# A hybrid decoder step on one core: projections behind two norms take centred, unscaled tiles, and the inverse deviation is applied to their results

## The chip, the core and the metric

One core of one Trainium2 chip runs the whole program. The metric is the device time of one execution in microseconds (us); smaller is better. Engines are named as in the profile: PE is TensorE (PEld its weight loads), DVE is VectorE, ACT is ScalarE, POOL is GpSimd, SP is SyncE, which issues the loads of the weights.

## What is computed

One inference step of a two-layer decoder for 256 prompt tokens and 8 sample tokens, with shared weights, in float32. The model width is 1024. Layer 0 is a gated DeltaNet mixer and a dense SwiGLU, layer 1 a short gated convolution and a mixture of eight experts. After each of the four parts the residual stream is normalised:

```
x = layer_norm(ALPHA * x + mixer(x))        # (x - mean) * rsqrt(var + 1e-5) * g + b
swiglu(x)    = (silu(x @ W_gate) * (x @ W_up)) @ W_down           # W_gate, W_up: 1024 x 2816
shortconv(x) = (B * conv3(C * h)) @ W_out,  [B, C, h] = x @ W_in  # W_in: 1024 x 3072
```

The change concerns two of the norms: that between the DeltaNet mixer and the SwiGLU (norm 0), whose result feeds `W_gate` and `W_up`, and that between the SwiGLU and the short convolution (norm 1), whose result feeds `W_in`.

## The kernel before

Activations lie transposed: 8 tiles `k` of 128 model rows by N = 264 columns (256 prompt and 8 sample tokens), in `xres`. Each fp32 product is made of three fp32r products: weights and activations are split into a high part (rounded to fp32r) and a low part (the rest), and high x high, high x low and low x high are summed. Weights come in slots of 1 MB. SP loads them up to seven slots ahead (`load`, L322 to L329, waits for the slot that had the place), ACT makes the high half of a slot (`split_high`, L331 to L336, three places, so slot n + 3 waits for slot n), DVE the low half (`split_low`, L338 to L342). PE works through a slot in `dense_slot` (L344 to L365): two output tiles, 16 products with the high half and 8 with the low half for each, 48 in all, and then raises `slot_used`.

The program is a written order for each engine; semaphores tie them. The stages are numbered by slot: four slots of `W_out` of the DeltaNet mixer (from `OUT0`), 22 of gate and up (`GU0`; pair i is a gate slot and an up slot of 256 columns each), 11 of `W_down` (`DOWN0`), 8 of C and h in pairs and 4 of B (`SCI0`), 4 of the convolution's `W_out` (`SCO0`), and then the experts (`MOE0`).

At norm l the order is a chain through three engines. DVE adds the residuals (L1183). PE sums the eight tiles against a matrix of ones, in 16 instructions, as each fp32 product is two (L1721). DVE makes `mu` (L1200) and subtracts it from each tile (L1203); ACT squares (L811); PE sums the squares (L1725); ACT makes `rstd` with a logarithm and an exponential, with the load of an activation table between them (L813, L815). Then, tile by tile, DVE scales by g and `rstd` (L1211), ACT adds b and rounds to `xh` (L818), DVE makes `xl` (L1207), and PE multiplies (L355, L356). ACT adds b to `xres` at the end (L821), for the next residual.

In the gate and up stage ACT applies silu to the gate bank (L838), DVE multiplies with the up bank (L1229), ACT and DVE split the product into `hh` and `hl` (L842, L1232), and both work on the sample states beside it: ACT scales the eight tiles of `dB` (L848), DVE updates `s0f` (L1239). In pairs 0, 1 and 2 PE also transposes eight blocks of `utail` into the banks of the next up slot (L1742) and waits until ACT has copied them out (L832, `tail_rows` after the change). The down stage starts when `hl` is complete. POOL starts the loads of the sample states when `xres` is final (L538).

## Time and profile before

| | us |
|---|---|
| median of 3 runs (1663.86 to 1668.59) | 1667.0 |
| the profiled execution | 1664.93 |
| its span, first to last instruction | 1663.2 |
| PE busy in the span | 1577.7 (95%) |
| DVE busy | 1273.1 (77%) |
| ACT busy | 1054.9 (63%) |
| POOL busy | 98.6 (6%) |

PE is the engine to look at: the share of the others is an average over stages with different limits. Matmuls are pipelined: a row gives the time from the start of the first to the modelled end of the last, so the distance between two starts is the price of what lies between them. Times of rows are us from the start of the span.

### The profile page before, as it was taken

What the parts mean: (1) busy time and instruction counts of PE and PEld (TensorE: products, weight loads), DVE (VectorE), ACT (ScalarE), POOL (GpSimd) and SP (SyncE); (2) the same over time, 40 slices, a digit from 0 to 9 for tenths busy, and PEclk for the clock granted to TensorE, in tenths of its full rate; (3) what the DMA queues carried; (4) which work ended last, traced back from release to release, by engine and by line L of the source; (5) the groups of instructions that cost most, each with busy time, mean ns of one, the idle gap of its engine ahead of it and who ended that gap; (6) DMA issues with size and microseconds to landing.
All of it is one profiled execution on the core that took longest, in us unless ns stands there. A gap on an engine that the chain in (4) does not pass through costs nothing.

```text
span 1663.2 us, 23648 instructions
## 1 busy us (share of the span) xinstructions
PE 1577.7 (95%) x8965; PEld 1367.2 (82%) x8965; DVE 1273.1 (77%) x1237; ACT 1054.9 (63%) x961; POOL 98.6 (6%) x155
## 2 busy tenths in 40 slices
PE   8899988999998999999999999999999999999991
PEld 7789987899997998887887887887887887887881
DVE  5786554567445758889889889889889889889887
ACT  5984233666334335777777777777777777777772
POOL 3105000121000011000000000000000000002001
PEclk9999998999998999999999999999999999999996
DMA  9747603598454545999999999999999999999991
GB/s 274 217 129 263 229 3 113 163 313 296 169 179 139 179 164 186 385 368 352 383 367 350 384 364 353 380 368 350 384 363 357 381 361 361 377 364 360 394 361 65
DMA packets 228401, 480.26 MB, mean 289 GB/s; under 512 B 9756, under 2 KB 69164, under 8 KB 228041
## 3 DMA queue, kind: packets, MB, share of 16 engines
q1 hardware_dynamic: 217000, 439.33, 74.1%
q0 software_dynamic: 11344, 40.12, 7.0%
q8 instruction: 41, 0.67, 0.2%
q14 instruction: 16, 0.13, 0.0%
HBM read 452.88 MB, written 26.77 MB: 288 GB/s over the span
## 4 chain that ended last, share of the span: by engine, by line
PE 88%; ACT 5%; DVE 4%; issue 1%; DMA 1%; DVEq 0%; SPq 0%; POOL 0%; ACTq 0%; POOLq 0%
PE bank L1866 13%; PE bank L1870 13%; PE bank L1867 13%; PE bank L1895 12%; PE bank L355 6%; PE bank L364 6%; PE bank L356 6%; PE bank L1901 6%; ACT high L336 2%; PE bank L1758 1%; PE bank L1759 1%; PE bank L1623 1%; PE bank L1764 1%; PE bank L1644 1%; PE bank L1878 1%
## 5 line engine op out<-in xcount | busy, mean ns | idle before, releaser
L341 DVE TENSOR_TENSOR low<-raw,high 128x2048 fp32r<-128x2048 f32 x408 | 931.1, 2290 | 244.3 <-ACT high L336 244.1
L336 ACT ACTIVATE high<-raw 128x2048 fp32r<-128x2048 f32 x408 | 779.8, 1917 | 284.3 <-PE bank L1870 103.2
L1866 PE MATMUL bank<-high,xgh 128*128 128x512 f32 x896 | 359.2, 401 | 0.7 <-DVE xgl L1419 0.7
L1867 PE MATMUL bank<-high,xgl 128*128 128x512 f32 x896 | 355.1, 396 | 0.0
L355 PE MATMUL bank<-xh,high 128*128 128x264 f32 x864 | 233.5, 301 | 15.6 <-ACT xh L818 7.7
L1870 PE MATMUL bank<-low,xgh 128*128 128x512 f32 x896 | 246.0, 396 | 0.0
L356 PE MATMUL bank<-xl,high 128*128 128x264 f32 x864 | 225.5, 293 | 0.0
L1870 PEld LDWEIGHTS bank<-low,xgh 128*128 128x128 f32 x896 | 168.9, 189 | 41.4
L1866 PEld LDWEIGHTS bank<-high,xgh 128*128 128x128 f32 x896 | 169.1, 189 | 39.5 <-issue 0.9
L1867 PEld LDWEIGHTS bank<-high,xgl 128*128 128x128 f32 x896 | 168.5, 188 | 38.7
L355 PEld LDWEIGHTS bank<-xh,high 128*128 128x128 f32 x864 | 169.8, 197 | 20.7 <-issue 20.7
L356 PEld LDWEIGHTS bank<-xl,high 128*128 128x128 f32 x864 | 170.4, 197 | 1.0 <-issue 1.0
L1895 PE MATMUL bank<-high,hth 128*128 128x512 f32 x448 | 141.4, 397 | 8.1 <-DVE htl L1435 8.1
L1895 PE MATMUL bank<-high,htl 128*128 128x512 f32 x448 | 140.5, 395 | 0.0
L364 PE MATMUL bank<-xh,low 128*128 128x264 f32 x864 | 129.8, 291 | 0.8 <-DVE low L341 0.8
L1901 PE MATMUL bank<-low,hth 128*128 128x512 f32 x448 | 122.3, 394 | 0.0
L364 PEld LDWEIGHTS bank<-xh,low 128*128 128x128 f32 x864 | 116.1, 193 | 1.1 <-DVE low L341 1.1
L1895 PEld LDWEIGHTS bank<-high,hth 128*128 128x128 f32 x448 | 83.5, 188 | 28.8 <-issue 10.0
L1901 PEld LDWEIGHTS bank<-low,hth 128*128 128x128 f32 x448 | 84.4, 188 | 20.2
L1895 PEld LDWEIGHTS bank<-high,htl 128*128 128x128 f32 x448 | 84.5, 189 | 19.8
L913 ACT ACTIVATE sgx<-bank 128x512 f32<-128x512 f32 x56 | 33.5, 598 | 42.6 <-PE bank L1870 42.5
L618 POOL TENSOR_TENSOR flag<-flag 128x1 f32<-128x1 f32 x1 | 2.3, 2255 | 873.7 <-DMA tok<-ysb 873.7
(370 smaller groups left out, 1463.9 us busy)
## 6 DMA issues: line engine op xcount, KB each, us to landing
raw<-in_moe_w_gu_dram SPq DMA_DIRECT2D x224, 1024.0 KB, 5.3
raw<-in_moe_w_down_dram SPq DMA_DIRECT2D x115, 1024.0 KB, 5.4
raw<-in_ffn_w_gu_dram SPq DMA_DIRECT2D x22, 1024.0 KB, 5.5
raw<-in_gdn_w_in_dram SPq DMA_DIRECT2D x16, 1024.0 KB, 9.1
tok<-zeros POOLq DMA_DIRECT2D x26, 512.0 KB, 18.2
raw<-in_sc_w_in_dram SPq DMA_DIRECT2D x12, 1024.0 KB, 5.0
raw<-in_ffn_w_down_dram SPq DMA_DIRECT2D x11, 1024.0 KB, 5.1
tok<-ysb SPq DMA_DIRECT2D x9, 512.0 KB, 5.9
```

The costliest lines, as they stand in the source:

```text
L336: eng.activation(high[:, n % SPLIT, :], raw[:, n % RAW, :], ACT.Copy).then_inc(high_ready, 1)
L341: eng.tensor_tensor(low[:, n % RAW, :], raw[:, n % RAW, :], high[:, n % SPLIT, :].bitcast(F32), ALU.subtract).then_inc(low_ready, 1)
L355: pe.matmul(out, wh[:, k, f], act_h[:, k, :], start=k == 0, stop=False)
L356: pe.matmul(out, wh[:, k, f], act_l[:, k, :], start=False, stop=False)
L364: last = pe.matmul(out, wl[:, k, f], act_h[:, k, :], start=False, stop=k == KT - 1)
L913: act.activation(sgx[:, u % 2, :], bank[2 * (u % 2)][:, :], ACT.Silu).then_inc(sgx_ready, 1)
L1623: last = pe.matmul(heads(4 * c + g)[:, h % 4, :], AT[:, c, h, :], T[:, c, h, :], start=True, stop=True)
L1866: pe.matmul(out, xgh[:, 4 * kh + k, :], wh[:, k, :], start=kh + k == 0, stop=False)
L1867: pe.matmul(out, xgl[:, 4 * kh + k, :], wh[:, k, :], start=False, stop=False)
L1870: last = pe.matmul(out, xgh[:, 4 * kh + k, :], wl[:, k, :], start=False, stop=kh == 1 and k == 3)
L1895: pe.matmul(bank[4 + g][:, :], src[:, u % 2, hs], wh[:, k, 512 * g:512 * g + 512], start=u + kh + k == 0 and src is hth, stop=False)
L1901: last = pe.matmul(bank[4 + g][:, :], hth[:, u % 2, hs], wl[:, k, 512 * g:512 * g + 512], start=False, stop=u == UNITS - 1 and kh + k == 2)
```

## The change

For a norm with z = x - mean, the projection W(z * rstd * g + b) is rstd * W(z * g) + W b, since `rstd` belongs to a column (a token) and not to a row. The kernel after uses this:

- The activation tiles get two more columns that hold b (N = 264, WIDE = 266), so that column 264 of each result is W b. `xh` and `xl` become the halves of z * g, made before the variance is known.
- The first slot behind each norm runs through `first_slot`, which goes by tile k through all products with `xh` first (two outputs, high and low weights), and then those with `xl`. The sum of squares follows this slot on PE.
- DVE multiplies each result by `rstd` out of the bank, and the column of W b is added in the silu (as its bias), in the identity of the C part, or in a `scalar_tensor_tensor` (up, h and B parts).
- `xres` is scaled by DVE (`norm_scale`) and shifted by ACT (`norm_shift`) later: two tiles in each of pairs 0 to 3 for norm 0, and around the slots of the convolution's `W_out` for norm 1.
- Most sums of the mean move into the slot before the norm. All `utail` transposes but the last eight come ahead of the first gate slot. POOL starts the state loads at the sums of the mean.
- ACT splits the next block before the gate work; DVE makes `hl` a pair later, except for the last pair; the first four banks of the down stage no longer wait for `hl` of the last pair; the last down slot is done output by output, so that residuals run beside it.
- In the convolution ACT makes the first of the three taps; the sums for `sgb` go behind the first slot of `W_out`, and that slot waits for `yl` tile by tile.

The core of the diff (sizes and places of the wide tiles, and the plain mirror lines of other stages, are left out):

```diff
+        def first_slot(pe, n, b, l):
...
+            for k in range(KT):
+                pe.wait_ge(xh_ready, halves_base(l) + k + 2)
+                for t in range(2):
+                    f = slice(128 * t, 128 * t + 128)
+                    pe.matmul(bank[b + t][:, 0:WIDE], wh[:, k, f], xhb[:, k, :], start=k == 0, stop=False)
+                    pe.matmul(bank[b + t][:, 0:WIDE], wl[:, k, f], xhb[:, k, :], start=False, stop=False)
+            for k in range(KT):
+                pe.wait_ge(xl_ready, halves_base(l) + k + 2)
+                for t in range(2):
+                    f = slice(128 * t, 128 * t + 128)
+                    last = pe.matmul(bank[b + t][:, 0:WIDE], wh[:, k, f], xlb[:, k, :], start=False, stop=k == KT - 1)
+            last.then_inc(slot_used, 1)
...
@@ gpsimd
-            pool.wait_ge(x_new, 8)
+            pool.wait_ge(mean_psum, 1)
@@ scalar
+            def norm_halves(l):
+                act.activation(xhb[:, :, N:WIDE], vecs[:, :, 4 + l:5 + l].to_broadcast([128, KT, 2]), ACT.Copy).then_inc(xh_ready, 1)
                 for k in range(KT):
                     act.wait_ge(xc_ready, 8 * l + k + 1)
+                    act.activation(xh[:, k, :], xres[:, k, :], ACT.Copy, scale=vecs[:, k, l:l + 1]).then_inc(xh_ready, 1)
+                for k in range(KT):
                     act.activation(lnsq[:, k, :], xres[:, k, :], ACT.Square).then_inc(lnsq_ready, 1)
...
+            norm_halves(0)
             act.wait_ge(hist_out, 48)
+            tail_rows(0)
+            tail_rows(1)
+            norm_scale(0)
             for i in range(FF // 256):
                 n = GU0 + 2 * i
+                if i == 2:
+                    tail_rows(2)
                 act.wait_ge(slot_used, n + 1)
                 split_high(act, n + SPLIT)
                 for t in range(2):
+                    act.wait_ge(gate_scaled, 2 * i + t + 1)
+                    g = sg[:, 2 * (i % 2) + t, :]
+                    act.activation(g[:, 0:N], g[:, 0:N], ACT.Silu, bias=g[:, N:N + 1]).then_inc(gate_silu, 1)
+                act.wait_ge(slot_used, n + 2)
+                if i < FF // 256 - 1:
+                    split_high(act, n + 1 + SPLIT)
+                    hidden_high(i)
+                else:
+                    hidden_high(i)
+                    split_high(act, n + 1 + SPLIT)
+                if i < KT // 2:
+                    norm_shift(0, 2 * i)
+                    norm_shift(0, 2 * i + 1)
                 if 1 <= i <= HEADS:
                     h = i - 1
                     act.wait_ge(sf_in[h % 2], 32 * (h // 2 + 1))
...
@@ vector
+            norm_halves(0)
+            split_low(dve, GU0 - 1 + SPLIT)
+            dve.wait_ge(var_root, 1)
             for i in range(FF // 256):
                 n = GU0 + 2 * i
                 dve.wait_ge(slot_used, n + 1)
+                for t in range(2):
+                    dve.tensor_tensor(sg[:, 2 * (i % 2) + t, :], bank[4 * (i % 2) + t][:, 0:WIDE], rstd[:, :], ALU.mult)\
+                        .then_inc(gate_scaled, 1)
+                if i:
+                    hidden_low(i - 1)
                 split_low(dve, n + SPLIT)
                 dve.wait_ge(slot_used, n + 2)
+                for t in range(2):
                     r = 2 * (i % 2) + t
+                    step(dve.tensor_tensor(hf[:, r, :], bank[4 * (i % 2) + 2 + t][:, 0:WIDE], rstd[:, :], ALU.mult))
+                step.wait()
+                for t in range(2):
+                    dve.wait_ge(gate_silu, 2 * i + t + 1)
+                    r = 2 * (i % 2) + t
+                    dve.scalar_tensor_tensor(hf[:, r, 0:N], hf[:, r, 0:N], hf[:, r, N:N + 1], sg[:, r, 0:N], ALU.add, ALU.mult)\
+                        .then_inc(h_ready, 1)
+                if i == FF // 256 - 1:
+                    hidden_low(i)
                 split_low(dve, n + 1 + SPLIT)
+                if i < KT // 2:
+                    norm_scale(0, 2 * i)
+                    norm_scale(0, 2 * i + 1)
...
@@ tensor
+                dense_slot(pe, n, 2 * (n % 2), xh, xl, out_arrives if n == OUT0 else None,
+                           half=(lambda: mean_sums(0, 0, 6)) if n == GU0 - 1 else None)
+            mean_sums(0, 6, KT)
...
             for i in range(FF // 256):
+                if i == 1:
+                    pe.wait_ge(var_inv, 1)
                 if i >= 2:
+                    pe.wait_ge(gate_scaled, 2 * (i - 1))
                     pe.wait_ge(h_ready, 2 * (i - 1))
+                for j in ((0, 1), (), (2,))[i] if i < 3 else ():
...
+                if i == 0:
+                    first_slot(pe, GU0, 0, 0)
+                    variance_sums(0)
+                else:
+                    dense_slot(pe, GU0 + 2 * i, 4 * (i % 2), xhb, xlb)
                 if i < 3:
+                    pe.wait_ge(tail_sb, 2 * (i + 1))
+                dense_slot(pe, GU0 + 2 * i + 1, 4 * (i % 2) + 2, xhb, xlb)
-            pe.wait_ge(hl_ready, FT)
             for n in range(DOWN0, SCI0):
...
+                pe.wait_ge(hl_ready, f + 2)
+                if n == SCI0 - 1:
+                    pe.wait_ge(low_ready, n + 1)
+                    for d in range(KT):
...
+                        last.then_inc(down_psum if d < KT - 1 else slot_used, 1)
+                        if d == KT - 2:
+                            pe.wait_ge(res_ready, 8 + 5)
+                            mean_sums(1, 0, 5)
+                    continue
+                for d in (4, 5, 6, 7, 0, 1, 2, 3):
+                    if n == DOWN0 and d in (4, 0):
+                        pe.wait_ge(h_ready, FT - 2 if d == 4 else FT)
...
```

DVE's `norm_halves` makes the low half of the two b columns (after a wait for ACT's first instruction above), `mu`, the eight centred tiles, and then the eight tiles of `xl` as `(x * g) - xh`. In the last slots before both norms ACT's `split_high` stands ahead of `norm_halves` in its order, as before.

## Rows read from the trace of the kernel before

**Rows 1.** The page: the chain that ended last, share by engine.

```profile
PE 88%; ACT 5%; DVE 4%; issue 1%; DMA 1%; DVEq 0%; SPq 0%; POOL 0%; ACTq 0%; POOLq 0%
```

**Rows 2.** Windows: stretch, length, busy us and instructions per engine, granted clock, DMA share, GB/s.

```profile
497.00:520.00 23.00, 14.37 (x49) 10.64 (x49) 14.83 (x34) 13.29 (x25) 0.11 (x1) 0.78 0.15 47
```

**Rows 3.** Timeline of PE and PEld at norm 0: start, length, line, idle before.

```profile
278.49 3.42 PEld L1721 LDWEIGHTS bank<-xres,ones 128*128 128x128 f32 x16
278.61 3.72 PE L1721 MATMUL bank<-xres,ones 128*128 128x264 f32 x16
284.45 5.51 PE L1725 MATMUL bank<-lnsq,ones 128*128 128x264 f32 x16 [2.12 <-ACT lnsq L811]
294.10 0.36 PE L355 MATMUL bank<-xh,high 128*128 128x264 f32 x1 [3.26 <-ACT xh L818]
...
310.15 0.86 PEld L1742 LDWEIGHTS bank<-ident,utail 128*11 128x11 f32 x8
```

**Rows 4.** Timeline of DVE and ACT at norm 0.

```profile
278.81 0.77 DVE L1183 SCALAR_TENSOR_TENSOR xres<-xres,bank 128x264 f32<-128x264 f32 x2 [1.53 <-PE bank L364]
283.05 0.42 DVE L1200 TENSOR_SCALAR mu<-bank 128x264 f32<-128x264 f32 x1
283.51 2.84 DVE L1203 TENSOR_TENSOR xres<-xres,mu 128x264 f32<-128x264 f32 x8
297.51 1.29 DVE L1207 SCALAR_TENSOR_TENSOR xl<-xres,vecs,xh 128x264 fp32r<-128x264 f32 x3
...
278.89 1.91 ACT L336 ACTIVATE high<-raw 128x2048 fp32r<-128x2048 f32 x1 [3.94 <-PE bank L364]
283.98 2.82 ACT L811 ACTIVATE lnsq<-xres 128x264 f32<-128x264 f32 x8 [1.87 <-DVE xres L1203]
290.50 1.28 ACT L815 ACT_TABLE_LOAD   x1
298.05 3.34 ACT L821 ACTIVATE xres<-xres,vecs 128x264 f32<-128x264 f32 x8
```

**Rows 5.** Timeline of DVE and ACT in pairs 1 and 2.

```profile
323.05 0.77 DVE L1229 TENSOR_TENSOR hf<-sg,bank 128x264 f32<-128x264 f32 x2 [0.99 <-PE bank L364]
326.11 2.29 DVE L341 TENSOR_TENSOR low<-raw,high 128x2048 fp32r<-128x2048 f32 x1 [1.37 <-ACT high L336]
328.45 2.19 DVE L1239 SCALAR_TENSOR_TENSOR s0f<-s0f,aS,dB 128x128 f32<-128x128 f32 x8
...
325.98 2.44 ACT L848 ACTIVATE dB<-dB,kS 128x128 f32<-128x128 f32 x8
328.32 1.05 ACT L832 ACTIVATE tail_nat<-bank 11x512 f32<-11x512 f32 x2
```

**Rows 6.** Timeline of PE at the start of the down stage.

```profile
428.23 1.13 PE L364 MATMUL bank<-xh,low 128*128 128x264 f32 x8
431.14 0.43 PE L1758 MATMUL bank<-hh,high 128*128 128x264 f32 x1 [1.78 <-DVE hl L1232]
438.64 0.29 PE L1758 MATMUL bank<-hh,high 128*128 128x264 f32 x1
```

**Rows 7.** Timeline of PE around norm 1 and before the slots of `SCO0`.

```profile
491.21 0.29 PE L1758 MATMUL bank<-hh,high 128*128 128x264 f32 x1
531.49 0.29 PE L355 MATMUL bank<-xh,high 128*128 128x264 f32 x1
591.12 1.04 PE L1781 MATMUL bank<-ident,su 128*10 128x128 f32 x8 [0.86 <-DVE sy L1289]
591.99 1.86 PE L1785 MATMUL bank<-gbw,ones 128*128 128x16 f32 x16
```

**Rows 8.** Windows of two us with the granted clock.

```profile
286.00:288.00 2.00, 2.00 (x6) 1.52 (x5) 0.34 (x1) 0.80 (x3) 0.00 (x0) 0.50 0.00 0
505.00:507.00 2.00, 0.55 (x3) 0.19 (x2) 1.56 (x5) 0.66 (x2) 0.00 (x0) 1.00 0.00 0
```

**Rows 9.** Chain in order of time, in the experts: start, length, what.

```profile
669.00 1.86 PE bank L1895 x8
```

More of the change, by code:

```diff
@@ L11 @@
 N = NP + NS
+WIDE = N + 2
 HEADS = 8
@@ L350, in dense_slot @@
                 f = slice(128 * t, 128 * t + 128)
-                out = bank[b + t][:, 0:N]
+                out = bank[b + t][:, 0:act_h.shape[2]]
                 for k in range(KT):
@@ L360, in dense_slot @@
                     pe.wait_ge(low_ready, n + 1)
+                elif half is not None:
+                    half()
                 for k in range(KT):
@@ L824, in _, with norm_shift, tail_rows @@
-            layer_norm(0)
+                act.activation(rstd[:, 0:N], rvar[:, :], ACT.Exp, scale=-0.5).then_inc(var_root, 1)
+            def norm_shift(l, k):
+                act.wait_ge(scaled, 8 * l + k + 1)
+                act.activation(xres[:, k, :], xres[:, k, :], ACT.Identity, bias=vecs[:, k, 4 + l:5 + l]).then_inc(x_new, 1)
+            def tail_rows(i):
+                for t in range(2):
+                    act.wait_ge(tail_psum, 2 * i + t + 1)
+                    act.activation(tail_nat[:, 1024 * i + 512 * t:1024 * i + 512 * t + 512],
+                                   bank[tail_bank(i) + t][0:11, :], ACT.Copy).then_inc(tail_sb, 1)
@@ L876, in _ @@
                 split_high(act, n + SPLIT)
+                for k in range(2 * (n - SCO0) + 2, min(2 * (n - SCO0) + 4, KT)):
+                    norm_shift(1, k)
             act.preload_act_table_set("natural_log")
@@ L1285, in _ @@
                 for t in range(2):
[L1286 to L1289 removed]
+                    step(dve.tensor_tensor(sy[:, 2 * (i % 2) + t, :], bank[2 * i + t][:, 0:WIDE], rstd[:, :], ALU.mult))
+                step.wait()
+                for t in range(2):
+                    f, y = 2 * i + t, sy[:, 2 * (i % 2) + t, :]
+                    dve.scalar_tensor_tensor(y[:, 0:N], y[:, 0:N], y[:, N:N + 1], sc[:, f, :], ALU.add, ALU.mult).then_inc(sy_ready, 1)
+                if i < D // 256 - 1:
+                    split_low(dve, n + SPLIT)
                 for t in range(2):
@@ L1302, in _ @@
             for n in range(SCO0, MOE0):
+                for k in range(2 * (n - SCO0) + 2, min(2 * (n - SCO0) + 4, KT)):
+                    norm_scale(1, k)
                 dve.wait_ge(slot_used, n + 1)
+                dve.wait_ge(x_new, 8 + 2 * (n - SCO0) + 2)
                 for t in range(2):
@@ L1710, in out_arrives, with mean_sums @@
                     pe.wait_ge(xl_ready, 8 + 4 + k // 2 + 1)
+            def mean_sums(l, first, end):
+                for k in range(first, end):
+                    pe.wait_ge(res_ready, 8 * l + k + 1)
+                    last = pe.matmul(bank[4][:, 0:N], ones[:, :], xres[:, k, :], start=k == 0, stop=k == KT - 1)
+                if end == KT:
+                    last.then_inc(mean_psum, 1)
             for n in range(OUT0, GU0):
@@ L1782, in _ @@
                 last.then_inc(stail_psum, 1)
-            pe.wait_ge(const_ready, 7)
-            for k in range(KT):
-                last = pe.matmul(bank[7][:, 0:16], ones[:, :], gbw[:, k, :, :].rearrange("p a e -> p (a e)"),
-                                 start=k == 0, stop=k == KT - 1)
-            last.then_inc(sgb_psum, 1)
             def row_tiles(k):
```

253 lines of the change are left out of this document (132 added, 121 removed).

## The prediction

> **What bounds the kernel now.** I read the chain that ended last first: PE holds 88% of it [rows 1]. In the gate, down and expert stages PE runs on end, and a cheaper DVE or ACT step there buys nothing. What can be bought is where PE waits, so I went through windows and then timelines for gaps. Before norm 1 and its first slot PE is busy 14.37 of 23.00 us, at a mean granted clock of 0.78 [rows 2]. Norm 0 looks the same [rows 3], the down stage starts with a short gap [rows 6], and one stands before the slots of `SCO0` [rows 7]. At a norm two things cost: the chain PE, DVE, ACT, PE, ACT, DVE, ACT, PE, and the clock, which falls to half (1.2 GHz) behind such gaps.
>
> **Unit prices on PE.** Nine down slots follow one another from 438.64 to 491.21 [rows 6, 7]: 52.57 / 9 = 5.84 us a slot of 48 products, 0.122 a product at 2.4 GHz. The first down slot took 438.64 - 431.14 = 7.50 [rows 6], 1.66 more: its first 16 products ran at 1.2 GHz, 0.10 more each, so a product costs 0.220 there. A sum instruction of a norm costs (3.72 - 0.39) / 15 = 0.222 at full clock (0.39 is the modelled drain of the last) [rows 3].
>
> **Norm 0.** I put zero at 278.49, where the low products of the last slot are out [rows 3]. Before, eight transposes end at 310.15 + 0.86 = 311.01, where pair 1 begins: 32.5 us. After:
> - Twelve sum instructions stand inside the last slot, 12 x 0.222 = 2.7, so the slot ends at 2.7. The residuals follow 0.32 later (278.81 - 278.49) and take 0.77 [rows 4]: 3.8. The last two sums end at 4.4. This alone gains nothing: the sums were hidden beside the residuals, and now the residuals wait for them.
> - ACT's `split_high` stands ahead of its first new instruction, from 3.1 to 5.0 (0.40 behind the slot's end, 1.91 long [rows 4]). The b columns on ACT and DVE cost 0.2 and 0.3 (small operations; none of this shape is in the rows, and L1200 at 0.42 bounds each from above, zero from below). `mu` starts at 5.5, before it was 283.05 - 278.49 = 4.6.
> - First centred tile 0.46 behind (283.51 - 283.05), ACT 0.47 behind that, PE 0.55 behind that (lnsq took 284.45 - 283.98 = 0.47; a scaled copy is some 0.08 longer) [rows 3, 4]: products from 7.0. The 16 transposes (2 x 0.86) fill 4.4 to 6.1, so PE has two short gaps of 1.0.
> - 32 products with `xh`, 3.9 at full clock: 10.9. ACT gives a tile each 3.34 / 8 = 0.42 [rows 4], PE eats four products per tile in 0.49: PE is the slower. `xl`: DVE is free at 5.9 + 2.84 = 8.8, and eight at (1.29 - 0.49) / 2 = 0.40 [rows 4] end at 12.0; PE ends at 12.3.
> - 16 sums, 3.6: 15.9. Up slot, 5.84: 21.7. `rstd` comes 2.3 behind the sums, beside that slot, and the table load of 1.28 [rows 4] is hidden there.
> Gain 32.5 - 21.7 = **10.8**. If the clock falls in these gaps, 17 `xh` products run at 0.220 and the `xl` products no longer wait for DVE: 14.5 instead of 12.3, a loss of 2.2. Nearest rows: a gap of 1.45 in the window at 505 left the clock at 1.00 [rows 8]; the gap of 2.12 at norm 0 was followed by 0.50 [rows 3, 8]. Gaps of 1.0 are nearer to the first; I take full clock.
>
> **Pairs 0 to 3.** ACT's order is now: split, two copies of `hh`, two shifts of `xres`, eight `dB`, and only then, at the head of pair 2, the copies of `tail_rows(2)`. The shifts wait for DVE's scaling, which stands behind a low split. PE waits for these copies before the up slot of pair 2. With zero at the end of pair 1's up slot: DVE `hf` from 0.3, 0.77 [rows 5]; `scalar_tensor_tensor` twice at 0.40, to 2.0; ACT's high half 0.3 to 2.2; low half 2.29 [rows 5], to 4.5; scales 4.9 and 5.4; shifts to 5.8; `dB` 2.44 less an overlap, to 8.2; copies 1.05, to 9.3 [rows 5]. PE is there at 0.86 + 5.84 = 6.7. **A stall of 2.5** in place of none: before, the same copies ended at 328.32 + 1.05 = 329.37, just when they were due. It is a gap longer than that of 1.78 at the down stage, behind which 16 products ran at 0.220 [rows 6]; I take 1.5 more for the clock. Bounds: 1.5 less each if DVE is quicker by its overlaps or the clock stays up. **Loss 4.0.**
> Nothing else of the stage reaches PE. DVE's round for pairs 1 to 3 is 0.77 + 0.78 + 2.29 + 0.77 + 0.85 + 2.29 + 0.85, then a wait for `dB` (2.4 + 0.4), then 2.19 [rows 5]: 13.6 against PE's 11.7. It falls behind by 1.9 a pair, but its latest product, the low half of slot n + 4, is due two slots and 16 products, 13.6, after the up slot and done at 4.5 plus the lag; the cover is 9, the lag at most 6, and from pair 4 the round is 11.0. `hl` a pair later costs nothing, for that reason. The last `utail` transposes stand before and after. State loads 20 us earlier meet idle DMA queues.
>
> At this point a rule of the Trainium skill would matter. No row shows a silu directly ahead of an identity; if identity lay outside silu's table, each of these pairs would pay 1.28 twice (the load row at 290.50 [rows 4]), and the stall would grow by 1.3. ScalarE: Activation LUTs, Table sets, says that cheap functions such as identity stand in every set; by it the term is zero.
>
> **Down stage.** Before, the low products of the last up slot are out at 428.23 + 8 x 0.122 = 429.21, the second down slot starts at 438.64: 9.43, 3.59 over 5.84 [rows 6]. After, 16 products (1.95) on banks 4 to 7 cover `hf` 0.3 + 0.77 and the two following, to 2.0. **Gain 3.4.**
>
> **Norm 1.** Zero at 491.21; before, 40.3 to 531.49 [rows 7]. After: seven outputs of six products, 5.1; ten sums, 7.3; the last output, 8.1; four sums beside the last residual, then two: 9.4. Here the residuals do run beside products. ACT's `split_high` again decides: 8.3 to 10.2, b columns to 10.8, then 0.46 + 0.47 + 0.55: products from 12.3. PE has idled 2.8 without transposes, so I take the low clock for 17 products as at the down stage: 12.3 + 3.7 + 1.8 = 17.8; 16 with `xl`, 19.8; sums, 23.3; slot, 29.2. **Gain 11.1**; 13.3 if the clock stays up (bounded then by `xl` at 17.3), 8.1 if it stays low through the first slot, as it did there before.
>
> **Behind it.** At `SCO0` the gap of 0.86 [rows 7] goes; the sums of `sgb` (1.7) only move behind the first slot; the last `yl` now holds tiles 6 and 7 by 0.3. **Gain 0.7** with rounding. `norm_scale` and `norm_shift` of norm 1 lie in idle time of DVE and ACT in the 5.84 of a slot; nobody waits before `SCO0 + 2`.
>
> **Wider tiles.** 34 slots x 48 products have two columns more. Rows: 8 products of 512 columns start (1.86 / 8) 0.2325 apart [rows 9], against 0.122 for 264: 0.445 ns a column, 0.9 ns a product, 1632 of them: **loss 1.45**.
> By TensorE: Matmul & The Clock Gate, Back-to-back issue gap, of the Trainium skill (N / 2.4 ns plus a constant), the loss is an estimated 1.36; its 112 ns for 264 columns is below the 122 of this trace.
>
> **Sum.** 10.8 - 4.0 + 3.4 + 11.1 + 0.7 - 1.45 = 20.5 us. The profiled execution took 1664.93 us, 1.7 above its span; 1664.9 - 20.5 = 1644.4. It lay 2.1 below the median of the three runs, 1667.0, so the median after is 1646.5. 0.3% (5 us) is about what a measurement of this kernel can tell from no change.
>
> **Rivals.**
> 1. The clock stays up and ACT reaches the copies in time: plus 2.2 (norm 1), plus 1.5 to 4.0 (pair 2): 1640.3 to 1642.8. For it: the gaps are short. Against it: both are longer than the 2.12 that was enough.
> 2. The clock falls at norm 0 too (2.2) and stays low through the first slot of norm 1 (3.0): 1651.7. For it: before norm 1 did just that; but there PE was fed by DVE at half load, now it is not.
> 3. Identity reloads tables: 1647.8 and up.
> 4. DVE becomes the bound of the gate and up stage. It now reads four banks a pair where it read two. If a read beside PE's writes cost double (1.54 more a pair), the round would be 15.1 in pairs 1 to 3 and 12.5 in pairs 4 to 8, over 11.7 by 3 x 3.4 + 5 x 0.8 = 14.2; less the cover of 9, 5 us: 1651.7. Against it: `hf`, with a bank operand, costs 0.77 for two, little more than tile operations without one (0.36 to 0.40 each) [rows 4, 5].
> 5. Slower: the width of 266 takes the products off their rate. The rows of such products have 264 or 512 columns, both multiples of eight. If the wide products of slots `GU0` to `SCO0` ran as slowly as the sums of the norms (0.222 for 264 columns), they would lose 1632 x 0.10 = 163 us: 1809. It outweighs the rest from 22 / 1632 = 0.0135 us a product. Against it: 264 and 512 columns both run at about 2.2 columns a ns (264 / 0.122, 512 / 0.2325), and nothing in the instruction changes but its count.
>
> **Chances.** Forecast 0.55 (its own range 1643.5 to 1649.5), rival 1 0.17, rival 2 0.15, rival 3 0.05, rival 4 0.04, rival 5 0.04; of rival 5 a quarter ends within 0.3%, and something unnamed may eat the gain. Faster 0.93, same 0.04, slower 0.03. The range for 8 in 10 takes in most of rivals 1 and 2: 1640 to 1653.
>
> **What would show it.** First `first_slot` product 7 us behind the moved origin at norm 0, without `rstd` before it; a PE gap of 2.5 in pair 2 released by ACT's `tail_rows`; no gap at the down stage; at norm 1 a gap of 2.8, `mu` right behind ACT's split, and a granted clock of 0.50 behind it; products of 266 columns 0.9 ns further apart. Wrong would be: PE waiting in pairs 3 to 10, which is DVE's round; or an unchanged gap before `SCO0`.

## The result, and the profile after

The changed kernel takes 1638.49 us (median of 4 runs, 1637.19 to 1639.28); the kernel before, in the runs made with it, 1667.8 (4 runs). The ratio is 0.983, 95% interval 0.981 to 0.985. Forecast were 1646.5 and a range down to 1640.0: the sign is right, the gain is larger than the range allows. The profiled execution took 1639.28 us against 1664.93 before. That is 25.65 us less, where the sum had 20.5. The missing 5 us are the question of this study.

The page of the kernel after (span 1637.6 us): busy time of each engine, and the chain that ended last, by engine.

```profile
PE 1560.2 (95%) x8965; PEld 1358.1 (83%) x8965; DVE 1295.6 (79%) x1301; ACT 1061.2 (65%) x971; POOL 100.2 (6%) x155
...
PE 87%; ACT 6%; DVE 4%; issue 1%; DMA 1%; DVEq 0%; SPq 0%; ACTq 0%; POOLq 0%
```

PE still holds the chain [rows 1]. The shares say nothing of where the time went, so I read the stages one by one, each from the same event in both traces.

**Norm 0**, timelines of PE, DVE and ACT (start, length, what, idle before and its releaser), against [rows 3, 4]:

```profile
278.04 2.84 PE L1816 MATMUL bank<-xres,ones 128*128 128x264 f32 x12
282.38 1.16 PE L1816 MATMUL bank<-xres,ones 128*128 128x264 f32 x4 [0.52 <-DVE xres L1247]
285.82 0.36 PE L359 MATMUL bank<-xhb,high 128*128 128x266 f32 x1 [0.53 <-ACT xhb L845]
289.84 2.14 PE L365 MATMUL bank<-xlb,high 128*128 128x266 f32 x16
291.82 3.72 PE L1830 MATMUL bank<-lnsq,ones 128*128 128x264 f32 x16
301.32 0.28 PE L379 MATMUL bank<-xhb,high 128*128 128x266 f32 x1
...
281.98 1.91 ACT L341 ACTIVATE high<-raw 128x2048 fp32r<-128x2048 f32 x1 [6.63 <-PE bank L390]
284.23 0.43 DVE L1269 TENSOR_SCALAR mu<-bank 128x264 f32<-128x264 f32 x1
```

The twelve sums stand ahead of the slot's last eight products (0.98 us) now. The zero of the prediction, the moment at which PE would be through the slot without them, is therefore 278.04 + 0.98 = 279.02. Pair 1 starts at 301.32, 22.3 behind; before it was 311.01 - 278.61 = 32.4 [rows 3]. The gaps of PE are 0.52 and 0.53, and the 32 products with `xhb` take 4.02 (285.82 to 289.84), so the clock stayed up.

**Pair 2**, timeline of PE, then windows (length; busy us and instructions of PE, PEld, DVE, ACT, POOL; granted clock; DMA share, GB/s):

```profile
318.99 1.15 PE L390 MATMUL bank<-xhb,low 128*128 128x266 f32 x8
322.41 0.59 PE L379 MATMUL bank<-xhb,high 128*128 128x266 f32 x1 [2.28 <-ACT tail_nat L863]
...
322.00:324.00 2.00, 1.59 (x7) 1.59 (x8) 2.00 (x9) 2.00 (x2) 1.15 (x3) 0.53 1.05 364
324.00:326.00 2.00, 2.00 (x13) 2.00 (x13) 2.00 (x4) 0.97 (x3) 0.87 (x1) 0.62 0.83 222
```

This is the foreseen stall, released by `tail_rows`, with the foreseen fall of the clock behind it. From 322.41 to the next slot at 329.82 it takes 7.41 us, where the slots of later pairs take 5.92: 1.5 us for the clock.

**Down stage and norm 1**, timelines of PE, DVE and ACT, against [rows 6, 7]:

```profile
423.56 1.15 PE L390 MATMUL bank<-xhb,low 128*128 128x266 f32 x8
424.54 0.28 PE L1877 MATMUL bank<-hh,high 128*128 128x264 f32 x1
...
485.72 2.29 DVE L346 TENSOR_TENSOR low<-raw,high 128x2048 fp32r<-128x2048 f32 x1 [3.90 <-ACT high L341]
487.93 2.46 DVE L1247 SCALAR_TENSOR_TENSOR xres<-xres,bank 128x264 f32<-128x264 f32 x7
489.76 2.49 PE L1816 MATMUL bank<-xres,ones 128*128 128x264 f32 x10 [1.37 <-DVE xres L1247]
492.82 1.50 PE L1816 MATMUL bank<-xres,ones 128*128 128x264 f32 x6
493.11 1.91 ACT L341 ACTIVATE high<-raw 128x2048 fp32r<-128x2048 f32 x1 [7.84 <-PE bank L1866]
495.33 0.43 DVE L1269 TENSOR_SCALAR mu<-bank 128x264 f32<-128x264 f32 x1
496.92 0.36 PE L359 MATMUL bank<-xhb,high 128*128 128x266 f32 x1 [2.59 <-ACT xhb L845]
500.93 2.14 PE L365 MATMUL bank<-xlb,high 128*128 128x266 f32 x16
512.41 0.28 PE L379 MATMUL bank<-xhb,high 128*128 128x266 f32 x1
```

The down stage starts right behind the last gate products. In its last slot DVE works on a low half (485.72 to 488.01) while seven banks wait for their residuals, and PE idles 1.37 us for it. The ten sums were meant to be hidden there. After the gap of 2.59 the 32 products take 4.01 (496.92 to 500.93), at full clock.

**Experts.** Their code is the same. Rows of one line, its first and last start: eight transposes of `xrow` for each of eight jobs, of before and then of after.

```profile
L1835 PE MATMUL bank<-ident,xrow x64: 272/273/273, 761.1 to 1622.4; 128*128 128x128 f32 x64
```

```profile
L1963 PE MATMUL bank<-ident,xrow x64: 272/273/273, 740.1 to 1596.6; 128*128 128x128 f32 x64
```

Seven periods took 861.3 us before and 856.5 after: 123.04 a job against 122.36. The chain in order of time (start, length, what) shows where, against [rows 9]:

```profile
647.67 0.93 PE bank L1998 x4
648.60 1.85 PE bank L2023 x8
650.45 0.91 PE bank L2029 x4
651.36 1.81 PE bank L2023 x8
```

Up products (L1998) need what they needed; down products (L2023, L2029), which have `hth` or `htl` as weights, are a little quicker: 1.81 to 1.85 for eight against 1.86. Over all 1344 of them, the median distance of two starts is 227 ns against 232; for the 2688 up products it is 234 in both traces. The granted clock is 1.00 in both. From the first expert product to the last instruction it makes 1012.1 us against 1017.4.

### The profile page after: what moved, and what is told of

Its sections match the earlier page's. It is cut to its first block, busy times and chain, and to the rows that moved or that the text cites. A ratio compares the mean times of both kernels' runs of the same rounds, so it can differ in the third digit from the quotient of the medians.

```text
span 1637.6 us, 23706 instructions
## 1 busy us (share of the span) xinstructions
PE 1560.2 (95%) x8965; PEld 1358.1 (83%) x8965; DVE 1295.6 (79%) x1301; ACT 1061.2 (65%) x971; POOL 100.2 (6%) x155
## 4 chain that ended last, share of the span: by engine, by line
PE 87%; ACT 6%; DVE 4%; issue 1%; DMA 1%; DVEq 0%; SPq 0%; ACTq 0%; POOLq 0%
PE bank L1995 13%; PE bank L1994 13%; PE bank L1998 13%; PE bank L2023 12%; PE bank L379 6%; PE bank L390 6%; PE bank L380 6%; PE bank L2029 6%; ACT high L341 2%; DVE low L346 1%; PE bank L1724 1%; PE bank L1745 1%; PE bank L2006 1%; PE bank L1877 1%; PE bank L1878 1%
## 5 line engine op out<-in xcount | busy, mean ns | idle before, releaser
L1998 PE MATMUL bank<-low,xgh 128*128 128x512 f32 x896 | 245.7, 396 | 0.0
L379 PE MATMUL bank<-xhb,high 128*128 128x266 f32 (+1 forms) x832 | 222.5, 299 | 10.3 <-ACT xhb L823 7.6
L380 PE MATMUL bank<-xlb,high 128*128 128x266 f32 (+1 forms) x832 | 215.7, 290 | 0.0
L1998 PEld LDWEIGHTS bank<-low,xgh 128*128 128x128 f32 x896 | 168.9, 188 | 41.1
L379 PEld LDWEIGHTS bank<-xhb,high 128*128 128x128 f32 x832 | 162.1, 195 | 12.5 <-issue 9.4
L380 PEld LDWEIGHTS bank<-xlb,high 128*128 128x128 f32 x832 | 161.4, 194 | 1.1 <-issue 1.0
L2023 PE MATMUL bank<-high,hth 128*128 128x512 f32 x448 | 140.0, 394 | 8.7 <-DVE htl L1536 8.7
L2023 PE MATMUL bank<-high,htl 128*128 128x512 f32 x448 | 138.6, 391 | 0.0
L390 PE MATMUL bank<-xhb,low 128*128 128x266 f32 (+1 forms) x832 | 124.8, 290 | 1.3 <-DVE low L346 1.3
L2029 PE MATMUL bank<-low,hth 128*128 128x512 f32 x448 | 119.9, 389 | 0.0
L390 PEld LDWEIGHTS bank<-xhb,low 128*128 128x128 f32 x832 | 110.8, 191 | 1.7 <-DVE low L346 1.6
L2023 PEld LDWEIGHTS bank<-high,hth 128*128 128x128 f32 x448 | 83.5, 188 | 28.2 <-issue 10.6
L2023 PEld LDWEIGHTS bank<-high,htl 128*128 128x128 f32 x448 | 84.1, 188 | 18.8
L2029 PEld LDWEIGHTS bank<-low,hth 128*128 128x128 f32 x448 | 84.1, 188 | 18.1
## 6 DMA issues: line engine op xcount, KB each, us to landing
raw<-in_gdn_w_in_dram SPq DMA_DIRECT2D x16, 1024.0 KB, 10.1
```

What stands on the lines that cost most here:

```text
L379: pe.matmul(out, wh[:, k, f], act_h[:, k, :], start=k == 0, stop=False)
L380: pe.matmul(out, wh[:, k, f], act_l[:, k, :], start=False, stop=False)
L390: last = pe.matmul(out, wl[:, k, f], act_h[:, k, :], start=False, stop=k == KT - 1)
L1998: last = pe.matmul(out, xgh[:, 4 * kh + k, :], wl[:, k, :], start=False, stop=kh == 1 and k == 3)
L2023: pe.matmul(bank[4 + g][:, :], src[:, u % 2, hs], wh[:, k, 512 * g:512 * g + 512], start=u + kh + k == 0 and src is hth, stop=False)
L2029: last = pe.matmul(bank[4 + g][:, :], hth[:, u % 2, hs], wl[:, k, 512 * g:512 * g + 512], start=False, stop=u == UNITS - 1 and kh + k == 2)
```

## The experiments

Ratios are to the kernel before, run on the same chip beside each.

### The region behind the operand tiles, moved by 128 bytes

The diff makes `xhb` and `xlb` 64 bytes a partition longer than `xh` and `xl` were. All that lies behind them in SBUF moves by 128 bytes, `hth` and `htl` too. This experiment gives the kernel before that move alone:

```diff
+        place("pad", [128, 32])
         region = cursor[0]
```

> The kernel before with one edit: an unused tile of 128 bytes a partition is placed ahead of the region whose tiles the expert stage uses (hth, htl, hx, sgx, ysb, xrow, the token tables). No instruction differs. In the change the same region moved by just these 128 bytes, because the two operand tiles became 266 columns wide, and a job of the expert stage (from one set of eight transposes of xrow to the next) took 122.25 us there against 122.9 us before. Address theory: the rate of the down products depends on where hth and htl lie, so this kernel's job period falls to 122.2 to 122.4 us, the expert stage from first product to last token store from 988.0 to about 982.7, and the time to about 1662 (0.997 of the kernel before). Rival, the difference has another cause (a run's chance, the chip, the order of work ahead of the experts): job period 122.9, time 1667, ratio 1.000.

Measured: 1662.14 us (10 runs), ratio 0.9968 (0.9955 to 0.9982).

```profile
L1836 PE MATMUL bank<-ident,xrow x64: 272/273/273, 762.6 to 1619.2; 128*128 128x128 f32 x64
```

856.6 us for seven periods, as in the changed kernel; the down products start 227 ns apart. The 5 us belong to an address, not to an order of work. (The profiled execution, 1661.97, also lost some 6 us to half clock just ahead of the experts; the end of "All together" comes back to it. The periods lie behind that.)

The same tile in the changed kernel moves the region on by another 128 bytes.

> The changed kernel with the same unused tile of 128 bytes ahead of the region, so that the region lies 256 bytes behind its place in the kernel before. Address theory with a period of 256 bytes: the slow job period of 122.9 us comes back, the time is 1638.5 + 5.2 = 1643.7 (ratio 0.986). Address theory with another period (any shift from the old place helps): 122.25 us stay and so does 1638.5. Rival, no part of it is the address: also 122.25 and 1638.5, but then the padded kernel before must show 122.9 as well.

Measured: 1641.81 us, 3.3 above the changed kernel; ratio 0.985 (0.982 to 0.987).

```profile
L1964 PE MATMUL bank<-ident,xrow x64: 272/273/273, 740.2 to 1601.5; 128*128 128x128 f32 x64
```

861.3 us: the slow period is back in full, with 232 ns between down products. In the traces that is 5.1 us from the first expert product on; the medians differ by less, since the four executions of this kernel alone scatter by 3. The forecast was made for such a kernel, and 1641.8 lies in its range.

### Only the two weight-side tiles

```diff
-        hth = place("hth", [128, 2, 512], F32R, at=region + 32 * D)
-        htl = place("htl", [128, 2, 512], F32R, at=region + 36 * D)
+        hth = place("hth", [128, 2, 512], F32R, at=region + 78 * D + 128)
+        htl = place("htl", [128, 2, 512], F32R, at=region + 82 * D + 128)
```

> The kernel before, with only the two weight-side operand tiles of the expert down products, hth and htl, placed elsewhere (in space that is free in that stage), so that their first byte lies at a multiple of 256 bytes from the arena's start instead of 128 bytes behind one; every other tile stays where it was, hx, sgx, ysb, xrow and xh too. In the trace of before a down product starts a median 232 ns after the one ahead of it, in the changed kernel 227 ns. Theory, it is the address of hth and htl: 227 ns, a job of 122.25 us, ratio about 0.997. Rival, it is the address of another tile of the region (hx, sgx or ysb, written by ScalarE and VectorE during the products): 232 ns, a job of 122.9, ratio 1.000.

Measured: 1660.57 us (10 runs), ratio 0.9971 (0.9956 to 0.9987); down products 227 ns apart; seven periods, 758.8 to 1615.4, 856.6 us. It is the address of `hth` and `htl`, and of no other tile. They lie far from their old place here; the padded kernel, where they move by 128 bytes only, has the same 227.

### The up products' tiles

If that is so, `xgh` and `xgl`, 96 bytes behind a multiple of 256 in both kernels, are in a slow place as well.

```diff
-        xgh = place("xgh", [128, KT, CAP], F32R, at=xs_at)
-        xgl = place("xgl", [128, KT, CAP], F32R, at=xs_at + 4 * D)
+        xgh = place("xgh", [128, KT, CAP], F32R, at=xs_at + 160)
+        xgl = place("xgl", [128, KT, CAP], F32R, at=xs_at + 160 + 4 * D)
```

> The changed kernel, with xgh and xgl, the weight-side operands of the experts' up products, 160 bytes further on, so that they lie at a multiple of 256 bytes instead of 96 bytes behind one. Their products start a median 234 ns apart in both kernels (2688 of them). Address theory, the start of the weight-side operand sets the rate: they come down to the 227 ns of the down products, 2688 x 7 ns = 18.8 us, a job of 119.9 us, time 1638.5 - 18.8 = 1619.7. Rival, their rate is set by something else (the 512-wide operand they share with the down products, or the ring's traffic in those slots): 234 ns and 1638.5 stay.

Measured: 1619.38 us (1618.02 to 1620.52), ratio 0.972 (0.970 to 0.975), 19.1 below the changed kernel. Chain in order of time, and the periods:

```profile
644.45 0.91 PE bank L1998 x4
645.36 1.81 PE bank L2023 x8
...
L1963 PE MATMUL bank<-ident,xrow x64: 272/273/273, 735.1 to 1575.4; 128*128 128x128 f32 x64
```

Four low up products take 0.91 in place of 0.93 or 0.94; the median is 227 ns in place of 234, a job 120.04 us in place of 122.36. Expected were 1619.7: the theory holds for tiles that it wasn't made from.

### Other distances, and the column side

> The changed kernel, with xgh and xgl at 64 bytes behind a multiple of 256, and hth and htl at 192 bytes behind one. The runs so far have 0 (227 ns between products of 512 columns), 96 (234) and 128 (232). Theory A, only a start at a multiple of 256 bytes is fast: up products 232 to 234 ns, down products 232 to 234; time 1638.5 to 1643.7. Theory B, a start at a multiple of 64 bytes is enough and 128 is special: up 227 and down 227, time 1619.4. Theory C, it grows with the distance to the next multiple: 64 and 192 alike, about 230, time about 1634.

> The changed kernel, with xgh and xgl at 128 bytes behind a multiple of 256, and hth and htl at 64. Theory A (only a multiple of 256 is fast) gives up 232 and down 232 to 234. Theory B gives up 232 and down 227. Theory C gives up 232 and down 230. If up products at 128 don't show the 232 ns that down products had there, the price hangs on the tile and not on the address alone. Time by A 1638.5 - 5.4 + 5 = 1638, by B 1633.

Measured, one run each: 1642.18 and 1639.01 us. Medians between starts, all runs together:

| start behind a multiple of 256 bytes | products | ns |
|---|---|---|
| 0 | down, up | 227, 227 |
| 64 | up, down | 233, 235 |
| 96 | up | 234 |
| 128 | down, up | 232, 232 |
| 192 | down | 231 |

Theory A holds in what it says of 0: by the medians the four other distances tried cost 4 to 8 ns, a multiple of 64 or 128 is not enough. Two of its sizes were missed by 1 ns (231 for 232 to 234, 235 for 232 to 234), and a median hides that the distances between products spread: by the mean, 192 costs less, 230.6 ns against 228.9 for down products at 0 in the changed kernel, 64 costs 5.1 (234.0). So the seven periods of the kernel with 64 and 192 take 856.6 us, no more than in the changed kernel, with 0.7 ns less on each of twice as many up products; its 1642.18 does not come from there. Each of these two kernels was run once. The weight loads themselves last a median 188 ns in every run, so no run shows how the address sets the pace. The distance is counted from the start of the kernel's arena in SBUF; where that lies is not known.

The next kernel has `xgh` aligned as above, and rows of `xhb` and `xlb` (the column side of the dense products) that each start at a multiple of 64 bytes. The diff without the moves that keep the other tiles in place:

```diff
+ROW = 272
...
+        place("ahead", [128, 8])
         xs_at = cursor[0]
-        xhb = place("xhb", [128, KT, WIDE], F32R)
-        xlb = place("xlb", [128, KT, WIDE], F32R)
+        xhb = place("xhb", [128, KT, ROW], F32R)[:, :, 0:WIDE]
+        xlb = place("xlb", [128, KT, ROW], F32R)[:, :, 0:WIDE]
...
```

> The changed kernel with xgh and xgl at a multiple of 256 bytes (as in the sixth experiment, 1619.4), and with the rows of xhb and xlb, the column-side operands of the 266-wide products, 1088 bytes apart instead of 1064, from a multiple of 128 bytes: each row then starts at a multiple of 64 bytes. The region behind keeps its place against multiples of 256. Theory, the column-side operand's start matters as the weight-side's does: the 2592 dense products (now 122 to 124 ns apart) come down by 2 to 4 ns, 5 to 10 us, time 1609 to 1614. Rival, only the weight-side operand's start matters: 123.7 ns between high products as now, time 1619.4.

Measured: 1619.43 us, the 1619.4 of the kernel without it. The distance between high products in the gate stage is a mean 124.0 ns against 123.7; a gate slot takes 5.933 us against 5.920, and just these two values also occur with one and the same gate code and tiles (5.920 in the changed kernel, 5.933 in the kernel with `xgh` at 128). On the column side this alignment is worth nothing. Nor is one to 256 bytes: rows 2 and 6 of `xhb` start at such a multiple here, and their low products are followed by the next after 124.3 ns, where the mean of the eight rows is 122.7; in the kernel before it is row 5 of `xh`, with 121.6 against 121.9. And the nine down slots behind the first, whose column-side tile `hh` moves by 128 bytes with the padding, take 52.57 us in the kernel before and 52.58 in the padded one.

### The stall in pair 2

```diff
-                if i == 2:
-                    tail_rows(2)
...
                     split_high(act, n + 1 + SPLIT)
+                if i == 1:
+                    tail_rows(2)
                 if i < KT // 2:
```

> The changed kernel, with ScalarE's last two tail_nat copies issued in round 1, behind hidden_high(1), instead of at the head of round 2 behind two norm_shift and the first eight dB activations. Theory: TensorE's stall of 2.28 us ahead of the up product at 322.41 and the fall of the granted clock to 0.53 and 0.62 in the 4 us behind it are both due to this queue place. The stall goes to under 0.3 us, the clock stays at 1.00, the time falls by 2.3 + 1.5 = 3.8 to 1634.7. Rival A, the clock falls anyway (it follows from the norm's gaps 30 us earlier): only 2.3 us come back, 1636.2. Rival B, the dB work then lies in the way of the next silu and the stall only moves to pair 2 or 3: 1638.5.

Measured: 1636.13 us, 2.4 below the changed kernel; the intervals of the two ratios overlap, so the traces have to show the gain. Windows at pair 2, then at norm 1:

```profile
322.00:324.00 2.00, 2.00 (x19) 2.00 (x18) 2.00 (x5) 0.93 (x2) 0.95 (x1) 1.00 0.56 189
...
492.00:494.00 2.00, 2.00 (x11) 2.00 (x10) 2.00 (x6) 2.00 (x6) 0.00 (x0) 0.50 0.03 8
```

The gap is gone and the clock is 1.00 there. From the first sums of norm 0 to the first product of the down stage it takes 418.90 - 276.33 = 142.6 us against 424.54 - 278.04 = 146.5: 3.9 less, for 3.8 expected. But in this execution the clock fell at norm 1 (last row), where the profiled run of the changed kernel had kept it: from the sums of the mean to those of the squares it took 1.5 us more. So the stall's price is as expected. In this execution the clock took some back elsewhere; whether that is why the median shows less, one profiled execution can't tell.

### The order around the norms

On ACT the b columns and `xh` go ahead of the last high half; on DVE the second to last low half of the down stage goes behind the norm's work (the diff shows DVE's part):

```diff
-                if n < SCI0 - 1:
+                if n < SCI0 - 2:
                     dve.wait_ge(slot_used, n + 1)
                     split_low(dve, n + SPLIT)
...
             norm_halves(1)
+            split_low(dve, SCI0 - 2 + SPLIT)
             split_low(dve, SCI0 - 1 + SPLIT)
```

> The changed kernel, with two moves around both norms. On ScalarE the norm's beta columns and the eight xh go ahead of the last split_high of the stage before (which then stands between the xh and the squares). On VectorE the second to last split_low of the down stage goes behind the norm's work, so that the residuals of the last down slot are not queued behind it. Theory: the 1.37 us stall before the ten sums of norm 1 goes, mu starts as the mean sums end instead of behind ScalarE's split: 0.8 us earlier in norm 0 and about 0.9 in norm 1, so 1.4 + 0.9 + 0.8 = 3.1 us in all, time 1635.4. Rival A: mu's wait was for the sums, not for the beta columns, and only the 1.4 come back, 1637.1. Rival B: the variance or the next slots' splits become late in their turn (splits end 4 us later), no gain, 1638.5.

Measured: 1636.27 us, 2.2 below the changed kernel, again with overlapping intervals. Timeline of PE and DVE at norm 1:

```profile
483.85 2.39 PE L1819 MATMUL bank<-xres,ones 128*128 128x264 f32 x10
486.81 1.50 PE L1819 MATMUL bank<-xres,ones 128*128 128x264 f32 x6
488.35 0.43 DVE L1271 TENSOR_SCALAR mu<-bank 128x264 f32<-128x264 f32 x1 [0.81 <-PE bank L1819]
489.94 0.36 PE L359 MATMUL bank<-xhb,high 128*128 128x266 f32 x1 [1.63 <-ACT xhb L845]
```

The ten sums follow without a gap, and `mu` waits for the sums and for nothing else. From the six sums to the first product 3.13 us pass instead of 4.10; with the 1.37 that is 2.3 at norm 1. At norm 0 the distance from the first sums to those of the squares falls from 13.78 to 13.13. The theory holds, with all three parts near their price. Some 0.4 of norm 0's part didn't reach the down stage (from the first sums to its first product 146.2 us against 146.5); most of that is the gate slots, 5.933 us each in this execution against 5.920. The profiled execution lies 4 us below the median of its kernel, and the first sums of norm 0 come 4.1 us earlier in it than in the changed kernel (273.96 for 278.04), ahead of all that the edit touches.

### The width

Columns 264 and 265 are not multiplied, so that what W b adds is left out of the results (one line of the diff stands for all):

```diff
-                dense_slot(pe, GU0 + 2 * i + 1, 4 * (i % 2) + 2, xhb, xlb)
+                dense_slot(pe, GU0 + 2 * i + 1, 4 * (i % 2) + 2, xh, xl)
```

> The changed kernel, with the dense products behind both norms 264 columns wide instead of 266: the two beta columns aren't multiplied, so the parts of the output that come from beta are wrong. Tiles, strides and everything else stay. It prices the width: 1632 products. By the sum of the prediction two columns cost 0.9 ns a product, 1.45 us in all: time 1637.0. By the starts read in the two traces (24 products in 2.965 us against 2.93) 1.5 ns, 2.4 us: 1636.1. If the changed row stride of the operand tiles (1064 bytes against 1056) is part of it, the period stays above the 122.1 ns of before, near 122.8, and only 1.2 us come back: 1637.3.

Measured: 1639.11 us (1635.27 to 1639.62), no less than with them. Low products in the first pairs, in the changed kernel and then here:

```profile
300.33 1.15 PE L390 MATMUL bank<-xhb,low 128*128 128x266 f32 x8
303.30 1.15 PE L390 MATMUL bank<-xhb,low 128*128 128x266 f32 x8
306.26 1.15 PE L390 MATMUL bank<-xhb,low 128*128 128x266 f32 x8
```

```profile
300.40 1.14 PE L391 MATMUL bank<-xhb,low 128*128 128x264 f32 x8
303.34 1.14 PE L391 MATMUL bank<-xhb,low 128*128 128x264 f32 x8
306.28 1.14 PE L391 MATMUL bank<-xhb,low 128*128 128x264 f32 x8
...
498.00:500.00 2.00, 2.00 (x11) 2.00 (x11) 2.00 (x7) 2.00 (x7) 0.00 (x0) 0.50 0.00 0
```

24 products take 2.965 and 2.94 us, so two columns cost 1.0 ns a product here, and 0.7 over the whole gate stage (123.23 against 122.57 us from slot to slot): the 0.9 of the sum lies between. Before, 24 took 2.93: some 0.4 ns came with the new tiles and not with the width; what of them does it stays open. The gain of 1.2 to 1.7 us doesn't show in the median. In the profiled execution the clock fell at norm 1 (last row, a window of this kernel), which took 1.5 us back; of the other three nothing of the kind is known.

### All together

The two orders, the tail rows and the aligned `xgh` in one kernel:

> The changed kernel with the tail rows moved (as in the third experiment), the two orders around the norms moved (as in the fourth) and xgh and xgl moved by 160 bytes. If the gains add: 2.4 + 2.2 by the medians of those two, and 18.8 by the address theory: 1638.5 - 23.4 = 1615.1. If the address theory fails for xgh: 1633.9. Rival, the two order gains overlap in the granted clock (each run had a spell of half clock somewhere else): up to 1.5 more, 1616.6.

Measured: 1617.4 us (1609.17 to 1618.4), 2.3 above what the gains add up to. Windows at the start of the experts:

```profile
612.00:614.00 2.00, 2.00 (x8) 1.55 (x7) 1.37 (x4) 0.52 (x1) 1.51 (x2) 0.50 0.58 221
618.00:620.00 2.00, 2.00 (x9) 1.55 (x9) 0.42 (x2) 0.00 (x0) 0.00 (x0) 0.50 0.00 0
```

The granted clock is 0.50 from 610 to 622, where the kernel with aligned `xgh` alone has 1.00. From the last product of the convolution's `W_out` to the first expert product it takes 31.2 us, in the kernel with aligned `xgh` alone 26.0. Three of the four executions have a mean clock of 0.980; the fourth, with 0.986, took 1609.17. Last, the same without the tail rows:

> The changed kernel with the norm order of the fourth experiment and xgh and xgl at a multiple of 256 bytes, the tail rows left where they are. In the eighth experiment all three together gave 1617.4 instead of 1615.1, and its profile has a spell of half clock of about 14 us at the start of the experts (granted clock 0.50 between 612 and 620), where the sixth has none. Theory, that spell comes and goes from run to run with the gaps of the router stage and doesn't belong to an edit: without it the gains of this pair add, 1619.4 - 2.2 = 1617.2, and single runs scatter by 3 or more. Rival, the spell belongs to the moved tail rows (the router stage then meets the clock at another phase): here it is gone in all runs and the time lies at 1617 with no run above 1619. Rival, the spell comes with the aligned tiles and the norm order together: 1619 to 1621.

Measured: 1615.17 us (5 runs, 1613.19 to 1615.72), ratio 0.970 (0.969 to 0.971); all five at a clock of 0.983 to 0.985, in the profiled one the window from 610 to 620 is at 1.00. This is the lowest median of the study, 50 us under the kernel before and 23 under the changed one; the intervals of the two ratios overlap (0.969, 0.966 to 0.973, with the tail rows moved), so which of the two kernels is faster isn't shown. Of nine executions three of four with the moved tail rows have the low clock, and none of five without, which speaks for the first rival. But the spell doesn't need these rows. The kernel before with the padding has it at the same place, without any of the moves (windows of its profiled execution):

```profile
632.00:634.00 2.00, 2.00 (x7) 1.55 (x8) 0.54 (x4) 0.00 (x0) 1.39 (x3) 0.50 0.60 244
640.00:642.00 2.00, 2.00 (x9) 1.55 (x8) 0.00 (x0) 0.00 (x0) 0.00 (x0) 0.50 0.00 0
```

There the same stretch takes 33.4 us, against 27.4 in the kernel before. And with the moved tail rows alone it is absent from the profiled execution (26.0 us). So the spell needs no moved tail rows, and coming and going from run to run, as the theory has it, fits these executions as well; whether an edit makes it more frequent, so few can't settle. PE was busy all through these windows, so no gap of PE within the spell explains it.

## Why the prediction was right and where it failed

Its steps against the two profiled executions (us; gains positive; each measured over the stretch of its stage, so the wider tiles are inside):

| step | predicted | measured |
|---|---|---|
| ahead of norm 0 | 0 | -0.4 |
| norm 0 to pair 1 | 10.8 | 10.1 |
| pairs 1 to 10 | -4.0 (-4.9 with width) | -5.0 |
| start of the down stage | 3.4 | 3.5 |
| norm 1 | 11.1 | 10.9 |
| behind norm 1, to the experts | 0.7 (0.2 with width) | 1.3 |
| experts | 0 | 5.3 |
| sum | 20.5 | 25.7 |

**The step that failed** is a term that the prediction put at nothing without a reason: the expert stage. It says of it only that PE runs on end there and that a cheaper step buys nothing; that code which isn't touched takes the time it took was taken for granted. The prediction priced instructions, waits and the clock, and under "Wider tiles" took the new tiles for a matter of 1632 products with two more columns. Their length moved the weight-side tiles of the expert stage to a multiple of 256 bytes, and 1344 products there became 4 to 5 ns shorter. The padded kernels show it in both directions. Take that away and the sum is 20.4 for 20.5, and the median 1641.8 for 1646.5. What is left of that last difference, 4.7 us, is in the step from the profiled execution to the median: the forecast added 2.1 for it, the padded kernel's profiled execution lies 2.1 above its median instead, and its whole gain was 21.0, 0.5 over the sum. Medians run side by side give the padded kernel a gain of 25.1 us (21.7 to 29.3), so some 4 us of it stand in no row of the table. The kernel before has executions of 1662.9 to 1667.5 us at a mean granted clock of 0.974 to 0.976 and others of 1668.5 to 1670.9 at 0.971 or 0.972, 31 and 11 of the 42 run beside the experiments, and its profiled one (0.975) is of the first kind; that this makes up the 4 us is likely, but not shown.

**Norm 0** came out 0.7 short, nearly all of it by a slip in the working: the 16 products with `xl` need 1.95 us behind the 32 with `xh`, so PE ends at 12.9 and not with DVE at 12.3. The steps ahead of it stand: first product 6.8 behind zero for 7.0, `xl` at 10.8 for 10.9 (289.84 - 279.02), full clock.

**Pair 2**: stall 2.28 for 2.5, clock 0.53 and 0.62 behind it for the 1.5 us taken; taking the cause away gave 3.9 back. Here the queue of ACT was read right, copy by copy.

**Down stage**: right to 0.1, no gap and full clock.

**Norm 1** was right by luck, by two errors that cancel. DVE's order in the last down slot wasn't looked at: `split_low` stands ahead of the residuals and cost PE 1.37; `mu` waited for ACT's split, as said. Against that, the clock stayed up behind a gap of 2.59, where half clock was taken for 17 products, 1.8 us. This was rival 1's case, in part. Of the eight profiled kernels that have this order of work at norm 1, and that gap, four lost the clock behind it and four kept it (from the sums of the mean to those of the squares 14.5 to 14.7 us in the first, 13.1 to 13.2 in the others), so rows of one execution could not have told which it would be.

**Behind norm 1**: the gap before `SCO0` went, and the products with tiles 6 and 7 of `yl` were late by some 0.1 each. Up to the last product of the convolution's `W_out` the stage takes 87.0 us, for 86.9 before, so it gained nothing where 0.2 was due. The 1.3 is clock, and luck: from there to the first expert product, with the router, it takes 26.0 us after and 27.4 before, while the profiled executions of two experiments, whose code in it is that of after and of before, took 27.4 (`xgh` at 64) and 33.4 (the padded kernel before).

**The wider tiles**: priced 0.9 ns, measured 0.7 to 1.0 for the width and some 0.4 for the tiles. Slots that took 5.86 us take 5.92 in the gate and up stage and 5.93 in the convolution: 2.2 us in place of 1.45. By TensorE: Matmul & The Clock Gate, Back-to-back issue gap, of the Trainium skill it would be an estimated 1.36; the runs agree with its 0.83 ns a product for two columns, and no part of that rule gives the other 0.4, nor a difference by address.

Rival 4 (DVE's round) and rival 5 (266 columns off the rate) show nowhere: no gap of PE in pairs 3 to 10, and the wide products start a mean 123.3 to 123.6 ns apart (a slot over 48). Rival 3 neither: silu and identity alternate without a table load between them.

## What to carry to other kernels

A change that resizes a tile moves all that is placed behind it; compare where the weight-side operands of TensorE start before and after, for the stages you didn't touch as well, and put them at a multiple of 256 bytes from a place known to be fast. Where a chain crosses engines, read each engine's whole queue at its ends, also for work that merely stands in the way: here two splits, one on ACT and one on DVE, cost 2.3 us at one norm. And a gain of a few us at one place can be taken or doubled by a spell of half clock elsewhere, so look at the clock of each stage before you credit an edit.

## What the runs showed of the hardware

- The start of the stationary operand in SBUF sets the pace of fp32r products 512 columns wide: 227 ns at a multiple of 256 bytes (from the arena's start), 231 to 235 at 64, 96, 128 and 192 behind one (medians). The weight load lasts 188 ns in all of them. For both stages of the experts together that is 24 us (5.3 and 18.5, the second from the job periods: 8 x 2.32).
- The start of the moving operand's rows doesn't: 124 ns between 266-wide products with rows 1064 and 1088 bytes apart, and no less at the rows that start at a multiple of 256 bytes (124.3 against a mean of 122.7).
- The granted clock can differ at the same place in the same order of work: behind a gap of about 2.6 us at norm 1 it stayed at 1.00 in four profiled kernels and fell to 0.50 in four. Ahead of the experts it is 0.50 for 14 us or more in two profiled executions of fourteen, with PE busy all the time. Single executions of the kernel before scatter over 8 us (1662.9 to 1670.9), the longest at the lowest mean clock (0.971 against 0.976).
